# Two chained transformer blocks on one core: X and Y products in turns on four quarters of the array, and keys, norm scale and activations of the convolution kept in PSUM

## The chip, the core and the metric

The kernel runs on one core of a Trainium2 chip. The metric is the device time of one execution in microseconds. The kernel before has a median of 1738.71 us over 3 runs (1736.97 to 1738.91).

## What is computed

Two blocks run one after the other on 512 rows of 1024 features, all in fp32. The reference, cut down:

```python
def first_block(x, mem, ...):
    h, mem_h = rms_norm(x, norm_g), rms_norm(mem, mem_norm_g)
    c_glu, c_gate, d_q, d_k, d_v, d_gate, x_q, x_gate, merge = split(h @ w_in)
    y_conv = conformer_conv_branch(...)        # conv over 31 rows, layer_norm, silu(u) * silu(gate), @ w_proj
    y_diff = differential_attention_branch(...)
    y_mem = memory_cross_attention_branch(...) # rms_norm of q and k, softmax over 256 rows of mem, * silu(gate)
    g = sigmoid(merge)
    return x + (g[0] * y_conv + g[1] * y_diff + g[2] * y_mem) @ w_out

def second_block(x, c, ...):
    mod = silu(c) @ w_ada + b_ada              # six rows that scale and shift
    p = (x * (1 + sc1) + sh1) @ w_in
    mix = concatenate([gmlp_spatial_gating(p), rwkv7_time_mix(p)]) @ w_out
    x = layer_norm(ALPHA * x + gt1 * mix)
    ...                                        # FFN with silu gate, layer_norm

def _rwkv7_step(S, inp):                       # scanned over 512 rows, 8 heads of 64 x 64
    r, w, k, v, a, b = inp
    sa = einsum('bhij,bhj->bhi', S, a)
    S = S * w + sa[..., None] * b + v[..., None] * k
    return S, einsum('bhij,bhj->bhi', S, r)
```

## The kernel before

Each of the engines TensorE, VectorE, ACT and GpSimd has a program written out by hand, and semaphores hold them together. Matrices are multiplied in split form: every operand is kept as a high part and a rest, and `mm3` (L564 to L566) issues three products, hi by hi, lo by hi and hi by lo. Weights come in an order that `unit_plan` lists. One unit is 128 x 1024 of weights, which is 8 blocks of 3 products, 24 in all. It lands in one of four `raw` slots. ACT makes its high part (`weight_hi`, L599) as soon as the unit three places before it has been used. GpSimd makes its rest (`weight_lo`, L607) in the first part of the kernel, and VectorE in the later part. Units named `ada` are pieces of `w_ada`: VectorE multiplies them by the silu of c and sums them (L620), and TensorE takes no part.

The products go to eight PSUM banks, which are handed round by rings: a ring is a list of banks, and a tile that takes a bank waits until the earlier holder is released.

The first part, until the convolution's projection: the depthwise convolution runs on VectorE as 240 multiply-adds (L1993, `bank<-conv_in,columns,bank`). In between and behind it VectorE scales the keys of the memory (4 heads, each a pair of 256-column tiles in one bank, ring of banks 6 and 7) into scratch in SBUF, ACT copies their high part (L1500, `k_x_hi`), VectorE subtracts it (L1998, `k_x_lo`). The convolution is centred, squared and summed. Its norm scale r goes to a scratch tile by an exponential. For each of 8 tiles ACT then makes the silu in a scratch tile (ring of three places), VectorE multiplies by the gate, ACT copies the high part (L1444), VectorE subtracts (`branch_lo`, L1998) and scales the tile after next by r (`normed`, L1990, `conv_out<-conv_out,scratch`). Meanwhile TensorE works through four units of cross attention's head 0: query 0, query 1, gate 0, gate 1, in banks 2, 0, 1 and 2. The sum of the query's squares (`query_sum`, L957) stands in the middle of gate 0. Behind that come the units of the convolution's projection, from bank 0 on.

The RWKV part works in chunks of 64 rows. For each of four features f (a pair of heads) two triangular matrices V and Y are built up in six levels (L1233 and the lines behind it); `pe_squares` (L1190) issues 8 x 2 products of 64 x 64, one for each of 8 chunks m and two lane halves. Levels 1 to 4 have three such groups: V, then X = Y by V, then Y = V by Y. ACT copies X and Y to SBUF, VectorE masks V. Features 0 and 1 take turns, and then 2 and 3. [...]

Of the kernel before, what the change touches and what calls it, by code (L numbers as in the profile page):

```python
# [67 lines left out]
def unit_plan():  # L68
# [38 lines left out]
    for h in range(X_HEADS):  # L107
        for c in range(2):
            f(("xq", 2 * h + c), "w_in", W_IN_AT["xq"] + (2 * h + c) * P)
            if h:  # L110
                a()
        for c in range(2):
            f(("x_gate", 2 * h + c), "w_in", W_IN_AT["x_gate"] + (2 * h + c) * P)
            if h:
                a()
        if h == 0:
            for d in range(KT):
                f(("proj", 0, d), "w_conv_proj", d * P)
                a()
                if d % 2:  # L120
                    a()
    project(1, "w_x_proj")
    for h in range(HEADS):
        f(("dq", h), "w_in", W_IN_AT["dq"] + h * P)
        a()
        f(("dk", h), "w_in", W_IN_AT["dk"] + h * P)
        if h in DV_AT:
            t(("dv", DV_AT[h]), "w_in", W_IN_AT["dv"] + DV_AT[h] * 512)
        f(("d_gate", h), "w_in", W_IN_AT["d_gate"] + h * P)
    project(2, "w_diff_proj")  # L130
# [138 lines left out]
def build(nc, dram, out):  # L269
# [169 lines left out]
    silu_ring, norm_ring, norm_ring_q = place_ring((6, 7, 10)), place_ring((8, 9, 0, 1)), place_ring((8, 9))  # L439
# [423 lines left out]
    def pe_conv_mean(pe, n):  # L863
        bank = stats.take(pe, "mean", conv_centred, KT - 1) if n == 0 else stats["mean"]
# [79 lines left out]
    def pe_cross(pe):  # L944
# [18 lines left out]
        for h in range(X_HEADS):  # L963
# [6 lines left out]
            later = h > 0  # L970
            feature_unit(pe, ("xq", 2 * h), unit_bank(pe, ("xq", 2 * h)), h_T, mid=first_scores if later else None)
# [7 lines left out]
            feature_unit(pe, ("x_gate", 2 * h), unit_bank(pe, ("x_gate", 2 * h)), h_T, mid=query_sum)  # L979
            if later:  # L980
                pe_cross_value(pe, h - 1, 0)
            feature_unit(pe, ("x_gate", 2 * h + 1), unit_bank(pe, ("x_gate", 2 * h + 1)), h_T,
                         mid=second_value if later else None)
# [201 lines left out]
    def pe_squares(pe, bank, lhs, rhs, start=True):  # L1185

        for m in range(8):
            for part in range(2):
                lanes = cut(part, CHUNK)
                done = pe.matmul(bank[lanes, cut(m, CHUNK)], lhs(m, lanes), rhs(m, lanes), start=start,  # L1190
                                 stop=start or m == 7)
        return done

# [18 lines left out]
    def pe_chunks(pe, f):  # L1212
# [18 lines left out]
        for level in range(6):  # L1231
# [8 lines left out]
            pe_squares(pe, bank, masked(0, 0), table(X) if level else identity, start=False).then_inc(*pe_c.up(f, "V", level))  # L1240
# [6 lines left out]
            if level < 5:  # L1247
                bank = wide.take(pe, ("X", f, level), act_c, f, "X", level)
            else:
                bank = wide.take(pe, ("LkV", f), act_c, f, "LkV")  # L1250
                pe.wait_ge(*dve_c.at(f, "masked", 1, 1))
                pe.wait_ge(*act_f.at(f, "tok", 3))
                pe_squares(pe, bank, masked(1, 0), rows_of(V_tok)).then_inc(*pe_c.up(f, "LkV"))
            pe.wait_ge(*(act_c if level > 1 else dve_c).at(f, "Y", level - 1))
# [232 lines left out]
    def act_keys(act):  # L1487
# [85 lines left out]
    def act_cross(act):  # L1573
# [35 lines left out]
        for h in range(X_HEADS):  # L1609
# [7 lines left out]
            if later:  # L1617
# [3 lines left out]
                turns(h - 1, 1)  # L1621
            feed_hi(act)
# [6 lines left out]
            feed_hi(act)  # L1629
            gate(h, 0)  # L1630
# [444 lines left out]
    def dve_key_full(dve, h):  # L2075
        dve.wait_ge(*norm_r.at("xk", h))
        for c in (1, 0):
            fused(dve, norm_ring["xk", h, c][:, 0:M], key_bank(h, c), column("x_kn_g", c),
                  norm_ring["xk", h, 0][:, 0:M], ALU.mult, ALU.mult).then_inc(*taken["dve"].up("xk", 2 * h + c))

    def dve_key_lo(dve, h):
        for c in range(2):
            dve_rest(dve, k_x[1][:, 2 * h + c, :], norm_ring["xk", h, c][:, 0:M], k_x[0][:, 2 * h + c, :],
                     norm_hi.at("xk", h, c)).then_inc(*norm_lo.up("xk", h, c))

    def dve_keys(dve):
# [5 lines left out]
        def normed(n):  # L2092
            mult(dve, conv[:, n, :], conv[:, n, :], conv_r_ring[0]).then_inc(*conv_normed.up(n))

        def gated(n):
            dve.wait_ge(*conv_silu.at(n))
            mult(dve, silu_ring[n], silu_ring[n], conv_gates[:, n, :]).then_inc(*conv_gated.up(n))
            if n + 2 < KT:
                normed(n + 2)
            if n:  # L2100
                dve_branch_lo(dve, "conv", n - 1, silu_ring[n - 1])
# [670 lines left out]
```

## Time and profile before

| what | value |
|---|---|
| median of the runs | 1738.71 us |
| the profiled execution's own time | 1738.34 us |
| its span | 1736.6 us |
| TensorE busy | 1627.2 us (94%) |
| VectorE busy | 1003.6 us (58%) |
| ACT busy | 723.5 us (42%) |
| GpSimd busy | 192.7 us (11%) |
| granted TensorE clock, mean | 0.978 |

The span is what the profile covers, and the kernel's own time is 1.7 us more. TensorE's share is a mean over all stages: where it is busy, only shorter work helps, and where it is not, the releaser of its wait counts.

### The profile page before, as it was taken

To read this page: it belongs to the slowest core of one execution; us is meant where nothing else is said; L and a number is where in the kernel's file an instruction comes from. 1 tells how busy PE (TensorE), PEld (TensorE's weight loads), DVE (VectorE), ACT (ScalarE), POOL (GpSimd) and SP (SyncE) were. 2 spreads that over 40 slices of the span, in tenths; PEclk is the share of its full clock that TensorE was granted. 3 is DMA by queue.
4 is the path that set the end of the run, shared out by engine and by line. 5 is a ranking of instruction groups with operands and counts; after the bars stand their busy time and mean duration, and the time that the engine had idled before them with its cause. 6 is when DMAs were issued, how large, how long until landed. Compare 5 with 4: busy or idle time off the path is not lost. (4 is left out here: it accounts for less than half of the span.)

```text
span 1736.6 us, 24246 instructions
## 1 busy us (share of the span) xinstructions
PE 1627.2 (94%) x9944; PEld 1283.6 (74%) x9944; DVE 1003.6 (58%) x1644; ACT 723.5 (42%) x1145; POOL 192.7 (11%) x158
## 2 busy tenths in 40 slices
PE   6999989999999999899999899999888999999995
PEld 5777776788787766677788686788666887887883
DVE  5999976666655476566444647675437443332227
ACT  5543346344522476467522635553325222222111
POOL 2343335400010000000005000000000000000000
PEclk9999999999999999999999999999989999999998
DMA  5222323654465322221333232200012332222321
GB/s 199 97 85 74 97 85 121 199 178 145 137 181 154 98 79 72 79 91 61 122 97 117 86 103 73 73 4 4 3 37 75 107 118 88 91 92 85 97 73 48
DMA packets 45644, 166.07 MB, mean 96 GB/s; under 512 B 5264, under 2 KB 5392, under 8 KB 45536
## 3 DMA queue, kind: packets, MB, share of 16 engines
q1 hardware_dynamic: 42912, 155.95, 28.0%
q0 software_dynamic: 2624, 8.59, 1.6%
q8 instruction: 79, 1.29, 0.3%
q14 instruction: 29, 0.24, 0.0%
HBM read 162.42 MB, written 2.10 MB: 95 GB/s over the span
## 5 line engine op out<-in xcount | busy, mean ns | idle before, releaser
L607 DVE TENSOR_TENSOR weight_lo<-raw,weight_hi 128x1024 fp32r<-128x1024 f32 x184 | 225.6, 1226 | 487.7 <-ACT weight_hi L599 487.7
L564 PE MATMUL bank<-h_T_hi,weight_hi 128*128 128x512 f32 x1208 | 496.3, 411 | 5.5 <-DVE h_T_lo L1998 3.4
L599 ACT ACTIVATE weight_hi<-raw 128x1024 fp32r<-128x1024 f32 x241 | 254.5, 1056 | 569.9 <-PE bank L566 567.2
L565 PE MATMUL bank<-h_T_lo,weight_hi 128*128 128x512 f32 x1208 | 480.2, 397 | 0.0
L566 PE MATMUL bank<-h_T_hi,weight_lo 128*128 128x512 f32 x1208 | 479.9, 397 | 0.0
L564 PEld LDWEIGHTS bank<-h_T_hi,weight_hi 128*128 128x128 f32 x1208 | 229.0, 190 | 70.7 <-issue 11.6
L565 PEld LDWEIGHTS bank<-h_T_lo,weight_hi 128*128 128x128 f32 x1208 | 228.8, 189 | 55.6 <-issue 5.6
L566 PEld LDWEIGHTS bank<-h_T_hi,weight_lo 128*128 128x128 f32 x1208 | 228.6, 189 | 55.2
L1993 DVE SCALAR_TENSOR_TENSOR bank<-conv_in,columns,bank 128x512 f32<-128x512 f32 x240 | 181.4, 756 | 8.3
L607 POOL TENSOR_TENSOR weight_lo<-raw,weight_hi 128x1024 fp32r<-128x1024 f32 x57 | 141.3, 2485 | 205.5 <-ACT weight_hi L599 205.5
L566 PE MATMUL bank<-branch_hi,weight_lo 128*128 128x512 f32 x192 | 75.9, 396 | 0.0
L564 PE MATMUL bank<-branch_hi,weight_hi 128*128 128x512 f32 x192 | 75.9, 396 | 0.0
L565 PE MATMUL bank<-branch_lo,weight_hi 128*128 128x512 f32 x192 | 75.9, 396 | 0.0
L564 PE MATMUL bank<-weight_hi,hidden_hi 128*128 128x512 f32 x176 | 70.4, 400 | 3.4 <-DVE scratch L1990 2.4
L620 DVE SCALAR_TENSOR_TENSOR raw<-raw,silu_row 128x1024 f32<-128x1024 f32 x48 | 69.5, 1452 | 5.9 <-DMA raw<-in_weights 5.9
L565 PE MATMUL bank<-weight_lo,hidden_hi 128*128 128x512 f32 x176 | 70.2, 399 | 0.0
L566 PE MATMUL bank<-weight_hi,hidden_lo 128*128 128x512 f32 x176 | 70.1, 398 | 0.0
L564 PE MATMUL bank<-weight_hi,h_T_hi 128*128 128x512 f32 x160 | 63.4, 396 | 3.0 <-DVE scratch L1993 3.0
L566 PE MATMUL bank<-weight_hi,h_T_lo 128*128 128x512 f32 x160 | 63.2, 395 | 0.0
L565 PE MATMUL bank<-weight_lo,h_T_hi 128*128 128x512 f32 x160 | 63.2, 395 | 0.0
L575 ACT ACT_TABLE_LOAD x45 | 57.7, 1283 | 3.4 <-issue 2.6
L752 POOL DMA_DIRECT2D ln_rows<-in_ln_g x4 | 2.2, 546 | 410.4 <-DVE scratch L1990 329.6
(442 smaller groups left out, 2324.2 us busy)
## 6 DMA issues: line engine op xcount, KB each, us to landing
raw<-in_weights SPq DMA_DIRECT2D x289, 512.0 KB, 3.5
x_in<-in_x SPq DMA_DIRECT2D x4, 512.0 KB, 5.4
x_rows<-in_x POOLq DMA_DIRECT2D x4, 512.0 KB, 4.9
out<-x_rows SPq DMA_DIRECT2D x4, 512.0 KB, 2.6
mem_in<-in_mem POOLq DMA_DIRECT2D x2, 512.0 KB, 8.0
ln_rows<-in_ln_g POOLq DMA_DIRECT2D x4, 256.0 KB, 3.9
ln_rows<-in_ln_b POOLq DMA_DIRECT2D x4, 256.0 KB, 4.5
silu_row<-in_c POOLq DMA_DIRECT2D x1, 512.0 KB, 11.0
```

The costliest lines, as they stand in the source:

```text
L564: pe.matmul(o, lhs[0], rhs[0], start=start, stop=False)
L565: pe.matmul(o, lhs[0], rhs[1], start=False, stop=False)
L566: return pe.matmul(o, lhs[1], rhs[0], start=False, stop=stop)
L575: return act.activation(o, i, func, bias=bias, scale=scale)
L599: act.activation(parts[n % SPLIT][0][:, :], raw[u % RAW][:, :], ACT.Copy).then_inc(*weight_hi.up(u))
L607: engine.tensor_tensor(lo[:, :], raw[u % RAW][:, :], view(hi[:, :]), ALU.subtract).then_inc(*ready.up(u))
L620: dve.scalar_tensor_tensor(out=slot, in0=slot, scalar=1.0, in1=silu_row[:, :], op0=ALU.mult, op1=ALU.mult, accum_out=mod[:, v, k:k + 1]).t ...
L752: pool.dma_start(ln_rows[half][:, :], dram[f"{name}_g"][:, cut(half, 512)].broadcast_to([P, 512])).then_inc(*rows_loaded.up(name, half, 0))
L1993: return dve.scalar_tensor_tensor(out=o, in0=a, scalar=scalar, in1=b, op0=op0, op1=op1)
```

## The change

It has four parts.

1. In the plan, head 0's units come in the order gate 0, query 0, query 1, gate 1. Four `ada` pieces leave the projection and stand behind the gate of every second head in the differential stage.
2. PSUM. The keys' ring gets a third bank (6, 7, 1); the keys are normed in their bank, read there for high part and rest, and the bank is free once the rest is made. The convolution's norm scale is written to bank 3, which held the mean. The silu tiles are in banks 6 and 7. ACT waits for the last centred tile before it writes the scale, and for the keys' last rest before the first silu. The rest of tile n-1 now comes ahead of the scaling of tile n+2 on VectorE.
3. `query_sum` stands in the middle of gate 1, and ACT makes the silu of gate 0 ahead of the query's squares.
4. In the RWKV levels 1 to 4, X and Y products alternate (`pe_level`) on four quarters of 64 x 64: X of a chunk's half reads one row half and writes one column half of its bank, and Y writes the other column half of another bank. V and Y are kept in the other half of the partitions from level 2 on (`crossed`, `turned`).

```diff
@@ unit_plan
     for h in range(X_HEADS):
-        for c in range(2):
+        if h == 0:
+            for name, n in (("x_gate", 0), ("xq", 0), ("xq", 1), ("x_gate", 1)):
+                f((name, n), "w_in", W_IN_AT[name] + n * P)
+        for c in range(2) if h else ():
...
             for d in range(KT):
                 f(("proj", 0, d), "w_conv_proj", d * P)
                 a()
-                if d % 2:
-                    a()
...
         f(("d_gate", h), "w_in", W_IN_AT["d_gate"] + h * P)
+        if h % 2 == 0:
+            a()
@@ rings
-    mem_places, key_places, key_sums = bank_ring((6, 7)), bank_ring((6, 7)), bank_ring((2,))
-    value_places, square_places = bank_ring((0, 1, 5, 4)), bank_ring((4,))
-    conv_places = ring([bank[:, :] for bank in banks[4:6]])
+    mem_places, key_places, key_sums = bank_ring((6, 7)), bank_ring((6, 7, 1)), bank_ring((2,))
+    value_places, square_places = bank_ring((0, 5, 1, 4)), bank_ring((4,))
+    conv_places, silu_ring = ring([bank[:, :] for bank in banks[4:6]]), ring([bank[:, :] for bank in banks[6:8]])
...
-    silu_ring, norm_ring, norm_ring_q = place_ring((6, 7, 10)), place_ring((8, 9, 0, 1)), place_ring((8, 9))
+    norm_ring, norm_ring_q = place_ring((8, 9, 0, 1)), place_ring((8, 9))
@@ TensorE
-        key_places.take(pe, ("xk", h), taken["dve"], "xk", 2 * h)
+        key_places.take(pe, ("xk", h), norm_lo, "xk", h, 1)
...
+            if h == 0:
+                feature_unit(pe, ("x_gate", 0), unit_bank(pe, ("x_gate", 0)), h_T)
...
             feature_unit(pe, ("x_gate", 2 * h + 1), unit_bank(pe, ("x_gate", 2 * h + 1)), h_T,
-                         mid=second_value if later else None)
+                         mid=second_value if later else query_sum)
...
+    def pe_level(pe, banks, Y, V, table, crossed):
+        for m in range(8):
+            for part in range(2):
+                rows = cut(part ^ crossed, CHUNK)
+                x_done = pe_square(pe, banks[0], table(Y), table(V), m, rows, cut(part, CHUNK))
+                y_done = pe_square(pe, banks[1], table(V), table(Y), m, rows, cut(1 - part, CHUNK))
+        return x_done, y_done
...
-            if level < 5:
-                pe_squares(pe, bank, table(Y), table(V)).then_inc(*pe_c.up(f, "X", level))
-            bank = wide.take(pe, ("Y", f, level), act_c, f, "Y", level)
-            pe_squares(pe, bank, table(V), table(Y)).then_inc(*pe_c.up(f, "Y", level))
@@ ACT
-                act.activation(k_x[0][:, 2 * h + c, :], norm_ring["xk", h, c][:, 0:M], ACT.Copy).then_inc(
-                    *norm_hi.up("xk", h, c))
+                act.activation(k_x[0][:, 2 * h + c, :], key_bank(h, c), ACT.Copy).then_inc(*norm_hi.up("xk", h, c))
...
-        act_root(act, r, square_places["conv_sq"], r, 1.0 / D, EPS5, conv_r.up())
+        act.wait_ge(*conv_centred.at(KT - 1))
+        act_root(act, stats["mean"], square_places["conv_sq"], r, 1.0 / D, EPS5, conv_r.up())
         values(0)
+        act.wait_ge(*norm_lo.at("xk", X_HEADS - 1, 1))
...
+            if h == 0:
+                gate(h, 0)
+                feed_hi(act)
             feed_hi(act)
             squares(h)
@@ VectorE
-            fused(dve, norm_ring["xk", h, c][:, 0:M], key_bank(h, c), column("x_kn_g", c),
+            fused(dve, key_bank(h, c), key_bank(h, c), column("x_kn_g", c),
...
-            dve_rest(dve, k_x[1][:, 2 * h + c, :], norm_ring["xk", h, c][:, 0:M], k_x[0][:, 2 * h + c, :],
-                     norm_hi.at("xk", h, c)).then_inc(*norm_lo.up("xk", h, c))
+            dve_rest(dve, k_x[1][:, 2 * h + c, :], key_bank(h, c), k_x[0][:, 2 * h + c, :],
+                     norm_hi.at("xk", h, 1)).then_inc(*norm_lo.up("xk", h, c))
...
-            mult(dve, conv[:, n, :], conv[:, n, :], conv_r_ring[0]).then_inc(*conv_normed.up(n))
+            mult(dve, conv[:, n, :], conv[:, n, :], stats["mean"]).then_inc(*conv_normed.up(n))
```

Three places of the order. First TensorE at head 0's query sum. Before, it stands in the middle of the third unit, gate 0, in bank 1 (`h_T` are the rows, `weight2` the third pair of weight slots):

```order
L566 MATMUL bank1<-h_T_hi_79,weight2_lo_58 128x512
L957 MATMUL bank3<-scratch_more0_86,ones_all_68 128x512
L957 MATMUL bank3<-scratch_more1_87,ones_all_68 128x512
L564 MATMUL bank1<-h_T_hi_79,weight2_hi_57 128x512
L565 MATMUL bank1<-h_T_lo_80,weight2_hi_57 128x512
```

With the change the same two products stand in the fourth unit, gate 1, in bank 2:

```order
L567 MATMUL bank2<-h_T_hi_79,weight0_lo_54 128x512
L958 MATMUL bank3<-scratch_more0_86,ones_all_68 128x512
L958 MATMUL bank3<-scratch_more1_87,ones_all_68 128x512
L565 MATMUL bank2<-h_T_hi_79,weight0_hi_53 128x512
L566 MATMUL bank2<-h_T_lo_80,weight0_hi_53 128x512
```

The sum has moved by one unit of 24 products; 12 products and no more lie between it and the projection.

Second, ACT in the silu loop, the last tiles. Before, silu goes to scratch tiles 6, 7 and more2 in turn, and the high part is read from there:

```order
L575 ACTIVATE scratch6_65<-conv_out_81,columns_70 128x512
L1444 ACTIVATE branch_hi_83<-scratch_more2_88 128x512
L599 ACTIVATE weight1_hi_55<-raw1_50 128x1024
L575 ACTIVATE scratch7_66<-conv_out_81,columns_70 128x512
L1444 ACTIVATE branch_hi_83<-scratch6_65 128x512
L599 ACTIVATE weight2_hi_57<-raw2_51 128x1024
L575 ACTIVATE scratch_more2_88<-conv_out_81,columns_70 128x512
```

With the change the same instructions write and read banks 6 and 7:

```order
L576 ACTIVATE bank7<-conv_out_81,columns_70 128x512
L1465 ACTIVATE branch_hi_83<-bank6 128x512
L600 ACTIVATE weight1_hi_55<-raw1_50 128x1024
L576 ACTIVATE bank6<-conv_out_81,columns_70 128x512
L1465 ACTIVATE branch_hi_83<-bank7 128x512
L600 ACTIVATE weight2_hi_57<-raw2_51 128x1024
L576 ACTIVATE bank7<-conv_out_81,columns_70 128x512
```

The order stays; three places have become two.

Third, TensorE at level 1 of feature 0. Before, X's 16 products come first and Y's 16 behind them:

```order
L1225 MATMUL bank4<-AR_161,k_T_162 64x128
L1225 MATMUL bank5<-AR_161,k_T_162 64x128
L1190 MATMUL bank6<-V0_166,Y0_167 64x64 x16
L1190 MATMUL bank7<-Y0_167,V0_166 64x64 x16
L1225 MATMUL bank0<-AR_161,k_T_162 64x128
```

With the change they alternate, 32 rows of which the first five:

```order
L1241 MATMUL bank5<-AR_161,k_T_162 64x128
L1190 MATMUL bank6<-V0_166,Y0_167 64x64
L1190 MATMUL bank7<-Y0_167,V0_166 64x64
L1190 MATMUL bank6<-V0_166,Y0_167 64x64
L1190 MATMUL bank7<-Y0_167,V0_166 64x64
L1190 MATMUL bank6<-V0_166,Y0_167 64x64
```

The number of products is the same, and X's result is complete one product ahead of Y's, where it was 16 ahead.

## Rows read from the trace of the kernel before

**Rows 1.** The page, part 1: busy us, share of the span, instructions.

```profile
PE 1627.2 (94%) x9944; PEld 1283.6 (74%) x9944; DVE 1003.6 (58%) x1644; ACT 723.5 (42%) x1145; POOL 192.7 (11%) x158
```

**Rows 2.** TensorE's waits, whole kernel: us in total, times, longest.

```profile
PE bank L564 <- DVE scratch L1993: 8.5, 2, 5.5
...
PE bank L957 <- ACT scratch_more L1590: 4.4, 1, 4.4
```

**Rows 3.** Stretches on TensorE: its busy us, granted clock, DMA share, GB/s.

```profile
core 0: us, PE busy (x), PEclk, DMA share, GB/s
...
239.76:245.54 5.78, 0.28 (x4) 0.77 0.22 82
...
245.54:249.54 4.00, 4.00 (x18) 0.50 0.00 0
...
287.70:301.70 14.00, 14.00 (x60) 1.00 0.36 114
```

**Rows 4.** Timeline of VectorE and GpSimd at the keys; line L1993, all.

```profile
230.13 4.92 POOL L607 TENSOR_TENSOR weight_lo<-raw,weight_hi 128x1024 fp32r<-128x1024 f32 x2 [4.29 <-ACT weight_hi L599]
...
231.29 4.04 DVE L1998 TENSOR_TENSOR k_x_lo<-scratch_more,k_x_hi 128x256 fp32r<-128x256 f32 x2
...
245.96 0.76 DVE L1998 TENSOR_TENSOR k_x_lo<-scratch,k_x_hi 128x256 fp32r<-128x256 f32 x2 [0.48 <-ACT k_x_hi L1500]
...
L1993 DVE SCALAR_TENSOR_TENSOR bank<-conv_in,columns,bank x240: 744/756/759, 35.9 to 243.9; 128x512 f32<-128x512 f32 x120
```

**Rows 5.** Timeline of VectorE and GpSimd in the silu loop.

```profile
279.38 8.18 POOL L607 TENSOR_TENSOR weight_lo<-raw,weight_hi 128x1024 fp32r<-128x1024 f32 x3 [4.68 <-ACT weight_hi L599]
...
280.04 2.43 DVE L1990 TENSOR_TENSOR scratch<-scratch,conv_gates 128x512 f32<-128x512 f32 x1 [0.36 <-ACT scratch L575]
...
293.86 2.89 DVE L1990 TENSOR_TENSOR scratch<-scratch,conv_gates 128x512 f32<-128x512 f32 x1
...
301.49 0.68 DVE L1998 TENSOR_TENSOR branch_lo<-scratch,branch_hi 128x512 fp32r<-128x512 f32 x1
```

**Rows 6.** Timeline of ACT, VectorE and TensorE at the query's root.

```profile
310.36 0.69 ACT L575 ACTIVATE scratch_more<-bank,eps 128x512 f32<-128x512 f32 x1 [3.45 <-PE bank L957]
...
311.81 1.41 DVE L1993 SCALAR_TENSOR_TENSOR scratch_more<-bank,x_gain,scratch_more 128x512 f32<-128x512 f32 x2 [6.77 <-ACT scratch_more L575]
...
315.37 1.28 ACT L575 ACT_TABLE_LOAD   x1
...
318.97 0.40 PE L564 MATMUL bank<-branch_hi,weight_hi 128*128 128x512 f32 x1
```

**Rows 7.** Timeline of VectorE in the differential stage.

```profile
639.34 1.22 DVE L620 SCALAR_TENSOR_TENSOR raw<-raw,silu_row 128x1024 f32<-128x1024 f32 x1
...
656.00 1.23 DVE L607 TENSOR_TENSOR weight_lo<-raw,weight_hi 128x1024 fp32r<-128x1024 f32 x1 [2.12 <-ACT weight_hi L599]
```

**Rows 8.** Timeline of TensorE in the RWKV part.

```profile
1143.09 1.10 PE L1190 MATMUL bank<-V,Y 64*64 64x64 f32 x32
...
1144.02 1.10 PE L1190 MATMUL bank<-Y,V 64*64 64x64 f32 x32
...
1174.69 0.33 PE L1295 MATMUL bank<-tok0v,tok0k 64*64 64x64 f32 x8
...
1174.81 0.32 PE L1293 MATMUL bank<-AL,LM0a 64*64 64x64 f32 x8
```

**Rows 9.** Timeline of VectorE and ACT between the levels.

```profile
1140.82 0.17 DVE L2508 COPY small<-scratch 128x8 f32<-128x8 f32 x1
...
1145.95 0.63 ACT L575 ACTIVATE scratch<-scratch 128x512 f32<-128x512 f32 x1 [4.37 <-DVE scratch L2516]
...
1159.47 0.74 DVE L1993 SCALAR_TENSOR_TENSOR f_kk<-k_T,columns,scratch 128x512 f32<-128x512 f32 x1
...
1164.63 0.68 DVE L1990 TENSOR_TENSOR V<-bank,levels 128x512 f32<-128x512 f32 x1
...
1227.85 0.63 ACT L1956 ACTIVATE y_b<-k_T 128x512 fp32r<-128x512 f32 x1 [1.35 <-DVE k_T L1990]
```

More of the change, by code:

```diff
@@ L119, in unit_plan @@
                 a()
-                if d % 2:
-                    a()
     project(1, "w_x_proj")
@@ L129, in unit_plan @@
         f(("d_gate", h), "w_in", W_IN_AT["d_gate"] + h * P)
+        if h % 2 == 0:
+            a()
     project(2, "w_diff_proj")
@@ L863, in pe_conv_mean @@
     def pe_conv_mean(pe, n):
-        bank = stats.take(pe, "mean", conv_centred, KT - 1) if n == 0 else stats["mean"]
+        bank = stats.take(pe, "mean", conv_normed, KT - 1) if n == 0 else stats["mean"]
         pe.wait_ge(*conv_done.at(n))
@@ L1183, in pe_tokens, with pe_square, pe_squares @@
                 yield
-    def pe_squares(pe, bank, lhs, rhs, start=True):
+    def pe_square(pe, bank, lhs, rhs, m, rows, lanes, start=True):
+        return pe.matmul(bank[lanes, cut(m, CHUNK)], lhs(m, rows), rhs(m, rows), start=start, stop=start or m == 7)
+    def pe_squares(pe, bank, lhs, rhs, start=True, crossed=False, turned=False):
         for m in range(8):
             for part in range(2):
-                lanes = cut(part, CHUNK)
-                done = pe.matmul(bank[lanes, cut(m, CHUNK)], lhs(m, lanes), rhs(m, lanes), start=start,
-                                 stop=start or m == 7)
-        return done
+                done = pe_square(pe, bank, lhs, rhs, m, cut(part ^ crossed, CHUNK), cut(part ^ turned, CHUNK), start)
+        return done
+    def pe_level(pe, banks, Y, V, table, crossed):
[5 more added lines that the diff above has]
+        return x_done, y_done
     def chunk_parts(f):
@@ L1239, in pe_chunks @@
                 pe.wait_ge(*act_c.at(f, "X", level - 1))
-            pe_squares(pe, bank, masked(0, 0), table(X) if level else identity, start=False).then_inc(*pe_c.up(f, "V", level))
+            pe_squares(pe, bank, masked(0, 0), table(X) if level else identity, start=False, turned=level > 1).then_inc(
+                *pe_c.up(f, "V", level))
             yield
@@ L1247, in pe_chunks @@
             if level < 5:
[L1248 to L1254, printed above, removed]
+                pair = wide.take(pe, ("X", f, level), act_c, f, "X", level), wide.take(pe, ("Y", f, level), act_c, f, "Y", level)
+                pe.wait_ge(*(act_c if level > 1 else dve_c).at(f, "Y", level - 1))
+                pe.wait_ge(*dve_c.at(f, "V", level))
+                x_done, y_done = pe_level(pe, pair, Y, V, table, level > 1)
+                x_done.then_inc(*pe_c.up(f, "X", level))
+                y_done.then_inc(*pe_c.up(f, "Y", level))
+                yield
+                continue
+            bank = wide.take(pe, ("LkV", f), act_c, f, "LkV")
+            pe.wait_ge(*dve_c.at(f, "masked", 1, 1))
+            pe.wait_ge(*act_f.at(f, "tok", 3))
+            pe_squares(pe, bank, masked(1, 0), rows_of(V_tok)).then_inc(*pe_c.up(f, "LkV"))
+            bank = wide.take(pe, ("Y", f, level), act_c, f, "Y", level)
+            pe.wait_ge(*act_c.at(f, "Y", level - 1))
             pe.wait_ge(*dve_c.at(f, "V", level))
-            if level < 5:
-                pe_squares(pe, bank, table(Y), table(V)).then_inc(*pe_c.up(f, "X", level))
-            bank = wide.take(pe, ("Y", f, level), act_c, f, "Y", level)
-            pe_squares(pe, bank, table(V), table(Y)).then_inc(*pe_c.up(f, "Y", level))
+            pe_squares(pe, bank, table(V), table(Y), crossed=True).then_inc(*pe_c.up(f, "Y", level))
             yield
@@ L1628, in act_cross @@
             query_hi(h)
-            feed_hi(act)
-            gate(h, 0)
+            if later:
+                feed_hi(act)
+                gate(h, 0)
             if later:
```

12 lines of the change are left out of this document (5 added, 7 removed).

## The prediction, made before the changed kernel ran

> **What bounds the kernel now.** I read the page first: TensorE is busy for 1627.2 us, 94% of the span of 1736.6 [rows 1]. So only two things move the time: a TensorE wait that shrinks, or TensorE work that gets shorter. The list of TensorE's waits came next. The wait for a key tile is 5.5 us in one piece and the wait for the query squares 4.4 us [rows 2]; the largest in the RWKV part is shorter. The table of stretches then shows what such a wait costs behind it: after the 5.78 us without work, the next unit takes 4.00 us at a granted 0.50 [rows 3]. At the full clock 14.00 us hold 60 products, 0.233 us each, so a unit of 24 is 5.6 us [rows 3]. A key product has half the columns, 0.117 us, so its unit of 24 is 2.8 us, and the half clock cost 1.2.
>
> **The key stage.** Key tile pair 3 is written to the bank that pair 1 holds; with three banks it takes the bank that pair 0 left. That removes the 5.5 us wait itself, but TensorE then waits for the weight of the second unit. How early is that? VectorE's lo of pair 0 took 4.04 us for two instructions while GpSimd split weights from 230.13, and 0.76 for the same two at 245.96 [rows 4]. All 240 instructions of the convolution, whose inputs are one tensor in SBUF, one in PSUM and a column, stay within 744 to 759 ns though GpSimd splits weights beside them [rows 4]. So an instruction with two inputs in SBUF is held up by GpSimd and one with a PSUM input is not. The keys' lo now reads PSUM: 3.3 us less, and with it comes all that stands behind it on VectorE and then on the others: the convolution's last 12 instructions, pair 1's keys, ACT's copy of them, the split of the weight that ACT does next, GpSimd's lo of it. The second unit, which starts at 249.54 in the stretch table [rows 3], can start 3.1 us earlier, at 246.4 (I leave 0.2 for the reads of PSUM). TensorE ends the first, 239.9 + 2.8, at 242.7 and waits 3.7 us; now the second unit runs at the full clock from 249.54 on, but after a wait of 3.7 us some of it may run at half. A full unit of that costs 1.2; I take 0.7, as the wait is shorter. Gain at the end of the keys: 3.1 - 0.7 = **2.4 us** (bounds 1.9 and 3.1).
>
> **The convolution's activations.** From 280.04 to 296.7 five of VectorE's instructions with two SBUF inputs are lengthened, the first to 2.43 us and the others to 2.89 as the last, against 0.68, while GpSimd works 8.18 us on three weights and more behind them [rows 5]. Excess: 2.43 + 4 x 2.89 - 5 x 0.68 = 10.6 us. ACT's silu waits for the scratch place that these free. With activations, norm scale and lo in PSUM every such instruction has one SBUF input, so the 10.6 us go. The last gated product of the loop ends at 301.5; without the excess it is near 291, and I take the same with two places in place of three, since each is handed on as soon as its two readers are done. The extra waits (last centred tile ahead of the root; last key lo ahead of silu 0; mean bank) are all met before the query units run: nothing.
>
> **The query stage.** The sum waits 4.4 us for ACT's squares [rows 2], which stand behind the silu loop; they are then early, made right after query 1. The sum sits in the middle of the fourth unit in place of the third. Units start at 287.70 - 2.4 = 285.3 [rows 3]; the sum begins at 285.3 + 3.5 x 5.6 = 304.9, and with 1 us for its two products ends at 305.9, the fourth unit at 308.7. But silu of gate 0 is now ahead of the squares, so the root needs a table load, which waits for the sum: 1.28 us for the load, 1.45 for logarithm and exponential (310.36 to 311.81), 1.41 for VectorE's two instructions, and 0.3 at each of four hand-overs: 311.2 [rows 6]. The convolution's first projection unit now takes bank 0, which VectorE's second instruction frees; before it starts, at 318.97, they are long done [rows 6]. So TensorE waits 2.5 us, and starts at **311.2 in place of 318.97: 7.8 us** for the whole first part. Upper bound: without that wait and without half clock at the keys, 7.8 + 2.5 + 0.7 = 11. Lower: the wait of 2.5 us is followed by as much lost to half clock, 5.3.
>
> **The moved pieces of w_ada.** Four leave the projection, where TensorE waits for none of them, and go to four heads of the differential stage. Each is 1.22 us of VectorE there [rows 7]. VectorE sits 2.12 us idle before the lo that follows [rows 7], so I take nothing. Without that cover it is 4 x 1.22 = 4.9 us slower. Their DMAs move with them, the same number.
>
> **The products X and Y.** 16 levels issue 32 of them each. The trace shows 32 records in 0.93 us (1143.09 to 1144.02), two records a product: 16 products, 58 ns each. They use two of four quarters of the array. Where this kernel has all four quarters in turns, in the chunks' outputs, the next line's 8 records start 0.12 us after the 8 before: four products take that, 29 ns each [rows 8]. So X and Y together go from 1.87 to 0.93 us, 16 x 0.93 = **14.9 us** at most. What the rest gives back, by the order of the instructions: for features 0 and 1 VectorE is at other work until 1140.99, and the first mask would be wanted some 0.5 us before; ACT's X copy stands behind an exponential at 1145.95 that waits for VectorE (1.35 us); and VectorE runs 5.2 us of other work from 1159.47 before the mask of level 5 (V at 1164.63), 1.6 us late [rows 9]. 7.5 - 0.5 - 1.35 - 1.6 = 4.1. For features 2 and 3 ACT copies y_b ahead of X at 1227.85 [rows 9]: 7.5 - 0.7 = 6.8. Together **10.9 us** (bounds: 14.9, and 7 if each of the 8 pairs of levels gave another 0.5 back).
>
> The Trainium skill speaks against this term: "TensorEngine Tiling (Array Packing)", section "Restrictions and Gotchas", has it that different row tiles cannot access the same PSUM bank at once. X's two parts come from two row halves, and write one bank, before and after. Rows 8 already show 58 ns for two row halves that write one bank; no row shows four quarters on two banks in which each bank is written from both row halves. By the rule nothing of the 14.9 us would come, which is rival B.
>
> **Sum.** 7.8 + 10.9 + 0 = 18.7 us off the span of 1736.6: 1717.9. The profiled run's own time is 1738.34, so 1719.6, and the median of the runs is 0.4 above that run: **1720.0 us**. No change within 0.2% is 3.5 us.
>
> **Rivals.**
> A, the forecast: 0.62. Own range by the bounds: 1738.7 - 25.9 = 1713 to 1738.7 - 12.3 = 1726.
> B, quarters in turns bring nothing, as matmuls from different row halves to one bank take turns: 7.8 alone, 1730.9. For it: no row has the case. Against it: 58 ns for two row halves in one bank [rows 8]. 0.10.
> C, the products halve but VectorE's and ACT's copies set the pace. A level needs V product, mask, X/Y product, two copies (0.69 + 0.6 + 0.6 us and hand-overs) and the X copy used to run beside the Y product. Then most of the 10.9 is lost: 1727 to 1731. Against it: two features take turns, so that a level of the other stands between a product and its copy's reader. 0.12.
> D, the moved pieces sit on VectorE's path in the differential stage: +4.9, 1725. 0.06.
> E, the other side: the four quarters don't overlap at all where both row halves share a bank in turns, and each product takes 117 ns in place of 58, as much as two. 512 x 58 ns = +30 us, so 1738.7 - 7.8 + 30 = 1761, slower. It decides from 58 + 7.8/512 = 73 ns a product on. Against it: every product row of the stretch is 58 or 29 [rows 8]. 0.05.
> F, the first part gains nothing (ACT into PSUM slower, two places too few, the wait at the projection long enough for half clock): 1738.7 - 10.9 = 1728. 0.05.
>
> **Range.** 1713 to 1731 holds A, B, most of C, D and F and leaves out E. Faster by over 0.2%: all but E and mishaps of several at once, 0.91; same 0.03; slower 0.06.
>
> **What would show it.** Right: rows of L1190's successor with X and Y at 29 ns a product (32 records each inside 0.93 us); no VectorE instruction of 2.9 us between 270 and 300; waits of 5.5 and 4.4 gone, one of about 3.7 before the last key unit, one of 2 to 3 at the first product of the projection, which starts near 311; in RWKV new waits on ACT's X copy and on V, about 4 us in all. Wrong: those RWKV waits at 8 us or more (C), spacing of 58 (B) or 117 (E); a VectorE wait of over 1 us more at each even differential head (D).

## The result, and the profile after

The changed kernel takes 1720.65 us (median of 4 runs, 1720.13 to 1721.15), the kernel before 1737.84 in the same comparison (4 runs). The ratio is 0.9901, 95% interval 0.9884 to 0.9918. The forecast was 1720.0 us, faster, with a range of 1713 to 1731.

The page of the changed kernel, part 1:

```profile
span 1718.6 us, 24264 instructions
...
PE 1610.7 (94%) x9944; PEld 1269.0 (74%) x9944; DVE 983.8 (57%) x1644; ACT 723.9 (42%) x1147; POOL 190.2 (11%) x158
```

TensorE is busy 16.5 us less than in [rows 1], VectorE 19.8 us less, and the span is 18.0 us shorter. The list of TensorE's waits in the changed kernel (us in total, times, longest; all lines have moved, L564 is now L565, L1993 is L2019, and L607 is L608):

```profile
PE bank L565 <- POOL weight_lo L608: 4.9, 4, 2.5
...
PE bank L1190 <- DVE V L2016: 4.0, 2, 3.0
...
PE bank L1320 <- issue: 3.0, 2, 2.1
PE bank L1190 <- issue: 3.0, 3, 1.4
...
PE bank L1314 <- issue: 1.5, 1, 1.5
...
PE bank L565 <- DVE scratch_more L2019: 1.4, 1, 1.4
...
PE bank L1190 <- DVE LM0k L2016: 1.1, 1, 1.1
```

The 5.5 and the 4.4 us of [rows 2] are gone. A wait for GpSimd's weight of 2.5 us and one of 1.4 us at the projection are there; both were forecast, at 3.7 and 2.5 us. Three rows say "issue", in which TensorE waits for nothing that the profile shows. They sum to 7.5 us, and two of their three lines are in the chunks' last products, the third among the level products. Before there were 3.8 us of them in the chunks. The forecast had no such term.

The first part, on the timeline of TensorE, VectorE and ACT of the changed kernel (start us, us, engine, line, instruction, idle before):

```profile
231.16 0.75 DVE L2024 TENSOR_TENSOR k_x_lo<-bank,k_x_hi 128x256 fp32r<-128x256 f32 x2
...
234.86 0.39 PE L565 MATMUL bank<-mem_T_hi,weight_hi 128*128 128x256 f32 x1 [0.69 <-ACT y_T L576]
...
246.19 0.58 PE L565 MATMUL bank<-mem_T_hi,weight_hi 128*128 128x256 f32 x1 [2.55 <-POOL weight_lo L608]
...
279.35 0.70 DVE L2016 TENSOR_TENSOR bank<-bank,conv_gates 128x512 f32<-128x512 f32 x1 [0.26 <-ACT bank L576]
279.96 0.68 DVE L2024 TENSOR_TENSOR branch_lo<-bank,branch_hi 128x512 fp32r<-128x512 f32 x1
280.56 0.68 DVE L2016 TENSOR_TENSOR conv_out<-conv_out,bank 128x512 f32<-128x512 f32 x1
...
291.55 1.28 ACT L581 ACT_TABLE_LOAD   x1
...
306.25 1.28 ACT L571 ACT_TABLE_LOAD   x1 [2.41 <-PE bank L958]
...
310.46 0.50 PE L565 MATMUL bank<-branch_hi,weight_hi 128*128 128x512 f32 x1 [1.45 <-DVE scratch_more L2019]
```

The rests of key pair 0 take 0.75 us in place of 4.04 [rows 4]. No instruction of the silu loop is lengthened (compare [rows 5]), and the loop is over at 291.55, when ACT loads its next table. The last key unit starts at 246.19, forecast 246.4. The projection starts at 310.46, forecast 311.2, before 318.97 [rows 6]. From the sum at 304.34 on, the path is ACT's table load behind the sum, root, VectorE, projection.

The row at 234.86 is a wait that the kernel before doesn't have and the forecast left out: ACT still reads the third bank of the keys, bank 1, for `y_T`, and the last four key units start 0.69 us late. The traces of the ten kernels below that have the third bank all show it, and those of e1_levels and e8_double_before, which have two, don't. The first part, as measured below, starts behind this wait.

In the levels X and Y products alternate. One pair of groups, the first of feature 1, begins so; its 64 records start from 1130.79 to 1131.73:

```profile
1130.79 0.24 PE L1190 MATMUL bank<-V,Y 64*64 64x64 f32 x1 [1.09 <-DVE LM0k L2016]
1130.80 0.27 PE L1190 MATMUL bank<-Y,V 64*64 64x64 f32 x1
1130.81 0.27 PE L1190 MATMUL bank<-V,Y 64*64 64x64 f32 x1
1130.81 0.27 PE L1190 MATMUL bank<-Y,V 64*64 64x64 f32 x1
1130.87 0.22 PE L1190 MATMUL bank<-V,Y 64*64 64x64 f32 x1
1130.90 0.22 PE L1190 MATMUL bank<-Y,V 64*64 64x64 f32 x1
```

64 records are 32 products, two records each, in 0.94 us: 29 ns each, half of the 58 in [rows 8].

**Where the 18.0 us came from, by the starts of the same instructions in both traces.** The projection begins 8.5 us earlier. From there to the chunks 0.75 is lost. The chunks (first product of AL to the last) take 112.5 us in place of 119.8: 7.2. Behind them another 1.9 is gained, and 1.2 more later on. The table of stretches of the changed kernel (us, TensorE's busy us, granted clock, DMA share, GB/s) has two places where the clock does it:

```profile
712.00:722.00 10.00, 8.39 (x30) 0.83 0.16 54
```

```profile
1233.70:1267.00 33.30, 24.64 (x171) 15.10 (x161) 11.34 (x26) 7.48 (x15) 0.00 (x0) 0.85 0.00 1
```

The first of them has 1.00 in the kernel before, and the second 0.76, in 35.1 us. Such stretches come out differently in the kernels below, which don't touch them: the second takes 33.1 us in e1_levels and 35.3 in e4_sbuf. They are the chance of one execution: the changed kernel profiled a second time (e12_again) takes 1.9 us longer in the second stretch, 4.1 us longer from the projection to the end, and has a span of 1721.5 against 1718.6.

### The profile page after: what moved, and what is told of

Read it like the earlier page. It is cut to its first block and busy times, and to the rows that moved or that the text cites. A ratio compares the mean times of both kernels' runs of the same rounds, so it can differ in the third digit from the quotient of the medians.

```text
span 1718.6 us, 24264 instructions
## 1 busy us (share of the span) xinstructions
PE 1610.7 (94%) x9944; PEld 1269.0 (74%) x9944; DVE 983.8 (57%) x1644; ACT 723.9 (42%) x1147; POOL 190.2 (11%) x158
## 5 line engine op out<-in xcount | busy, mean ns | idle before, releaser
L608 DVE TENSOR_TENSOR weight_lo<-raw,weight_hi 128x1024 fp32r<-128x1024 f32 x184 | 225.5, 1225 | 485.0 <-ACT weight_hi L600 485.0
L565 PE MATMUL bank<-h_T_hi,weight_hi 128*128 128x512 f32 x1208 | 496.4, 411 | 4.5 <-DVE h_T_lo L2024 2.4
L565 PEld LDWEIGHTS bank<-h_T_hi,weight_hi 128*128 128x128 f32 x1208 | 229.7, 190 | 66.9 <-issue 10.3
L2019 DVE SCALAR_TENSOR_TENSOR bank<-conv_in,columns,bank 128x512 f32<-128x512 f32 x240 | 181.4, 756 | 8.3
L608 POOL TENSOR_TENSOR weight_lo<-raw,weight_hi 128x1024 fp32r<-128x1024 f32 x57 | 138.6, 2437 | 199.9 <-ACT weight_hi L600 199.8
L565 PE MATMUL bank<-branch_hi,weight_hi 128*128 128x512 f32 x192 | 76.0, 396 | 1.4 <-DVE scratch_more L2019 1.4
L565 PE MATMUL bank<-weight_hi,hidden_hi 128*128 128x512 f32 x176 | 69.7, 396 | 3.4 <-DVE scratch L2016 2.4
L565 PE MATMUL bank<-weight_hi,h_T_hi 128*128 128x512 f32 x160 | 64.1, 401 | 3.0 <-DVE scratch L2019 3.0
L621 DVE SCALAR_TENSOR_TENSOR raw<-raw,silu_row 128x1024 f32<-128x1024 f32 x48 | 64.3, 1341 | 1.7 <-DMA raw<-in_weights 1.7
```

The lines of the kernel that those rows point to most:

```text
L565: pe.matmul(o, lhs[0], rhs[0], start=start, stop=False)
L608: engine.tensor_tensor(lo[:, :], raw[u % RAW][:, :], view(hi[:, :]), ALU.subtract).then_inc(*ready.up(u))
L621: dve.scalar_tensor_tensor(out=slot, in0=slot, scalar=1.0, in1=silu_row[:, :], op0=ALU.mult, op1=ALU.mult, accum_out=mod[:, v, k:k + 1]).t ...
L2019: return dve.scalar_tensor_tensor(out=o, in0=a, scalar=scalar, in1=b, op0=op0, op1=op1)
```

## The experiments

Three numbers stand for each run. "First part" is from the start of the last four key units on TensorE to the first product of the projection, "chunks" is the stretch above; both are from its trace.

| run | median us | first part | chunks | issue waits in the chunks |
|---|---|---|---|---|
| before | 1737.84 | 84.8 | 119.8 | 3.8 |
| changed | 1720.65 | 75.6 | 112.5 | 7.5 |
| e1_levels | 1727.34 | 83.9 | 112.0 | 6.6 |
| e2_first | 1732.10 | 75.8 | 120.3 | 4.4 |
| e3_grouped | 1727.97 | 74.3 | 116.3 | 4.3 |
| e4_sbuf | 1729.46 | 81.6 | 112.8 | 6.3 |
| e5_order | 1717.03 | 73.1 | 111.7 | 6.5 |
| e6_ada | 1721.58 | 75.7 | 111.4 | 7.2 |
| e7_double | 1747.66 | 75.6 | 138.1 | 17.7 |
| e8_double_before | 1764.24 | 83.5 | 149.5 | 3.7 |
| e9_table | 1717.24 | 73.0 | 111.6 | 6.7 |
| e10_feed | 1713.94 | 70.3 | 112.1 | 7.0 |
| e11_keys | 1725.25 | 79.2 | 112.1 | 7.7 |
| e12_again | 1721.35 | 75.6 | 113.0 | 6.4 |

The kernel before had a median of 1737.92 us in the comparison with e1 to e4, 1738.87 with e5 to e8 and 1739.00 with e9 to e12. The chunks take 111.4 to 113.0 us in all the kernels with undoubled products in turns, so a difference below about 1.5 us there isn't to be read.

### The levels alone, and the rest alone

e1_levels is the kernel before with `pe_level`, `crossed` and `turned`; e2_first is the changed kernel without them.

> The kernel before with part 4 alone (X and Y in turns on four quarters). If the parts are independent, as the forecast has it, this gives what the changed kernel gains between the first level and the end of the chunks, 7 to 9 us: about 1729.5 us. Rival (code): the chunks' stretch shows waits of 1 to 2 us without a releaser, 7 us in all in place of 3.8, each a multiple of 256 TensorE instructions after the one before. Rival (levels need the earlier start of the first part): under 4 us gained, above 1734.

> The changed kernel with X and Y as before (part 4 taken back). Independent parts: the projection starts at about 310.5 as in the changed kernel, the levels are as before, time 1729.5 to 1730.5. Rival (the gain of the first part is given back at half clock later): 1733 or more.

e1: 1727.34 us, ratio 0.9950 (0.9932 to 0.9968). The chunks are 7.7 us shorter, the first part is as before. That is the forecast's separation, with the medians 2 us below the expectation: the profiled run again has some 2 us of clock behind the chunks. The issue waits are 6.6 us, as the rival about code has it. e2: 1732.10 us, ratio 0.9966 (0.9953 to 0.9979), first part 9.0 us shorter and chunks as before. Of these 9 us only about 6 are in the median: the projection begins 7.9 us earlier than before, and by the first product of the chunks 1.6 of that are lost again. That stretch takes 809.0 to 811.9 us over all fourteen traces, 0.6 more in e12_again than in the first profile of the same kernel. The two ratios together give 0.9916, against 0.9901 (0.9884 to 0.9918) for both: independent within the intervals. Rival B (no gain in the products) is out.

### What the turns do, and what the layout

e3_grouped keeps the other half of the partitions but issues all X products first:

```diff
     def pe_level(pe, banks, Y, V, table, crossed):
         for m in range(8):
             for part in range(2):
                 rows = cut(part ^ crossed, CHUNK)
                 x_done = pe_square(pe, banks[0], table(Y), table(V), m, rows, cut(part, CHUNK))
+        for m in range(8):
+            for part in range(2):
+                rows = cut(part ^ crossed, CHUNK)
                 y_done = pe_square(pe, banks[1], table(V), table(Y), m, rows, cut(1 - part, CHUNK))
```

> The changed kernel with V and Y in the other half of the partitions, but all 16 X products ahead of the 16 Y products. If the turns of the four quarters are what pays: 58 ns a product again and the time of the kernel without part 4, about 1729 to 1731. Rival (the layout itself, or X and Y overlap without turns): as the changed kernel, 1720 to 1722.

The expectation was wrong. The chunks take 116.3 us: 4.0 of the 7.8 us between e2 and the versions in turns are there without any turns. TensorE's timeline of this run, two features' levels one behind the other:

```profile
1142.99 0.97 PE L1190 MATMUL bank<-V,Y 64*64 64x64 f32 x26
1143.75 0.27 PE L1190 MATMUL bank<-Y,V 64*64 64x64 f32 x2
...
1143.92 0.80 PE L1190 MATMUL bank<-Y,V 64*64 64x64 f32 x21
1144.54 0.27 PE L1190 MATMUL bank<-V,Y 64*64 64x64 f32 x2
...
1144.71 0.80 PE L1190 MATMUL bank<-V,Y 64*64 64x64 f32 x21
1145.30 0.27 PE L1190 MATMUL bank<-Y,V 64*64 64x64 f32 x2
```

Where X's group ends, Y's products already start among X's last ones, since they use the other two quarters: a group takes 0.76 to 0.79 us in place of 0.93. Two groups are 1.55 us, against 1.87 before and 0.93 in turns. So 16 x 0.32 = 5.1 us is the layout's nominal part and 16 x 0.62 = 9.9 that of the turns; 4.0 and 3.8 arrive. Of what is missing from the turns, 3.2 us are issue waits (7.5 in the changed kernel, 4.3 here), to which the next experiment turns.

### Is it code that the short products wait for?

TensorE's "issue" waits have no releaser. I counted TensorE's instructions in the trace (weight loads, products, and the semaphore instructions between them) from one to the next:

```
changed:          1138.30 -> 1168.42: 1791   -> 1187.76: 1024   -> 1195.31: 512    -> 1229.10: 1793   -> 1233.27: 255
e12_again:        1137.9  -> 1169.2:  1791   -> 1195.9:  1536   -> 1229.3:  1793   -> 1233.2:  255
```

All are multiples of 256, give or take one. The DMA view shows code arriving in pieces of 16 KB; its row for one of the queues, for the whole of the changed kernel and then of e7_double (described below), is:

```profile
q8 instruction: 79, 1.29, 0.3%
```

```profile
q8 instruction: 87, 1.43, 0.3%
```

That queue is TensorE's: TensorE has 20355 instructions in the changed kernel, 79.5 times 256, and e7_double has 2048 more, 8 times 256.

e7_double and e8_double_before issue every X and Y product of levels 1 to 4 twice, into the same place:

```diff
 e7, pe_level
-            for part in range(2):
+            for part in (0, 1, 0, 1):
 e8, pe_chunks
+                pe_squares(pe, bank, table(Y), table(V))
                 pe_squares(pe, bank, table(Y), table(V)).then_inc(*pe_c.up(f, "X", level))
             bank = wide.take(pe, ("Y", f, level), act_c, f, "Y", level)
+            if level < 5:
+                pe_squares(pe, bank, table(V), table(Y))
```

> The changed kernel with every X and Y product of levels 1 to 4 issued twice into the same place (512 more products). If loading of code sets the pace where products are short, the waits without a releaser grow from 7.5 us to 15 or more, each a multiple of 256 instructions behind the last, and the chunks take over 18 us longer. If those waits are something else, the chunks take 12 to 15 us longer (512 x 29 ns = 14.9, less waits for data that it covers) and these waits stay near 7.

> The kernel before with every X and Y product of levels 1 to 4 issued twice. Products take 58 ns there, so 256 instructions, 64 products, take 3.7 us. Both theories: 27 to 31 us more. Code loading: waits without a releaser stay under 6 us, as a block of instructions lasts about as long as it takes to come. If the products are cheaper than 58 ns when they follow each other at once: under 25.

Waits of e7_double on TensorE around the chunks, and the code in its DMA view of the same 142 us:

```profile
PE bank L1190 <- issue: 13.7, 12, 1.8
...
PE bank L1320 <- issue: 2.5, 2, 1.5
PE bank L1314 <- issue: 1.5, 1, 1.5
```

```profile
q8 instruction: 32, 0.52, 1.6%
```

The chunks take 25.6 us more than in the changed kernel, where the products alone are 14.9. Issue waits are 17.7 us in 15 pieces, and the counts between them are 512, 256, 512, 767, 1024, 1025, 255, 512, 256, 768, 512, 512, 513 and 255. Where two follow at once (1140.8 and 1144.7, 1200.8 and 1204.6, 1212.3 and 1216.3, 1256.3 and 1259.9) the 256 instructions take 3.6 to 4.0 us, wait included, though 64 products of 29 ns are 1.9 us. In e8_double_before 64 products of 58 ns are 3.7 us, the chunks take 29.7 us more (512 x 58 ns = 29.7), and the issue waits stay at 3.7. (Its median is only 25.4 us above the kernel before, under the 27 expected: some 4 us came off in the first part and behind the chunks, which the edit doesn't touch.)

So a block of 256 TensorE instructions takes about 3.8 us to come, and products of 29 ns use it up in half the time. That the block is fetched code follows from counts, rate and the size of the pieces, and from when the pieces start. In all fourteen traces every issue wait in the chunks, over 80 together, ends 2.2 to 2.9 us after the latest piece has started, and in e7_double, between waits that follow at once, a piece starts every 3.6 to 4.0 us. The issue wait of 5.2 us that every trace has behind the chunks is no such wait: it ends 14 to 16 us after a piece, and 338 instructions behind the wait before it in the changed kernel. Still, no run changed the fetching itself.

The Trainium skill, "Runtime: NRT & Kernel Launch", section "Instruction fetch mechanics", has the block (16 KiB, 256 instructions), and this trace agrees. It also says that the fetch is hidden, because instructions are issued more slowly than they arrive. This case's trace doesn't agree: TensorE waits 7.5 us of the chunks, and 17.7 with the products doubled.

### Is it GpSimd, and PSUM?

e4_sbuf puts the silu tiles back into SBUF, three places; the norm scale stays in PSUM. e11_keys puts the scaled keys back; banks and releases stay as changed.

```diff
 e4
-    conv_places, silu_ring = ring([bank[:, :] for bank in banks[4:6]]), ring([bank[:, :] for bank in banks[6:8]])
+    conv_places = ring([bank[:, :] for bank in banks[4:6]])
+    silu_ring = place_ring((6, 7, 10))
 e11
-            fused(dve, key_bank(h, c), key_bank(h, c), column("x_kn_g", c),
+            fused(dve, norm_ring["xk", h, c][:, 0:M], key_bank(h, c), column("x_kn_g", c),
 (key_hi and dve_key_lo read norm_ring["xk", h, c] in place of key_bank(h, c))
```

> The changed kernel with the silu tiles back in SBUF, three places; the norm scale stays in PSUM. If GpSimd holds up VectorE instructions with two SBUF inputs, several of the gated products and rests between 275 and 300 take 2.4 to 2.9 us again, the silu loop ends 4 to 8 us later and the projection starts 3 to 6 us later: 1723 to 1727. Rival (it is the order and the squares' early place, not PSUM, that bought the time): within 1 us of the changed kernel.

> The changed kernel with the scaled keys in SBUF again (banks and releases stay). If GpSimd holds up an instruction with two SBUF inputs: the two rests of pair 0 take 4 us in place of 0.75, the last key unit waits 5 to 6 us in place of 2.55, and 2 to 3.5 us are lost, 1723 to 1724. Rival (only the third bank mattered): within 1 us of the changed kernel.

VectorE's timeline of e4_sbuf:

```profile
276.76 2.29 DVE L2016 TENSOR_TENSOR scratch<-scratch,conv_gates 128x512 f32<-128x512 f32 x1 [0.36 <-ACT scratch L576]
278.97 2.89 DVE L2024 TENSOR_TENSOR branch_lo<-scratch,branch_hi 128x512 fp32r<-128x512 f32 x1
281.79 0.67 DVE L2016 TENSOR_TENSOR conv_out<-conv_out,bank 128x512 f32<-128x512 f32 x1
282.38 2.29 DVE L2016 TENSOR_TENSOR scratch_more<-scratch_more,conv_gates 128x512 f32<-128x512 f32 x1
```

and TensorE's waits of the same run between 236 and 330 us:

```profile
PE bank L565 <- DVE v_x_lo L2024: 3.5, 1, 3.5
PE bank L565 <- DVE scratch_more L2019: 1.4, 1, 1.4
```

Five instructions take 2.3 to 2.9 us, and all five have two inputs in SBUF. The scaling by the norm scale, one input of which is now in PSUM, takes 0.67 to 0.68 each time, between them and in the same kernel. The loop ends some 5 us later, VectorE's rest of the values with it, and the third unit waits 3.5 us for the bank that it frees, at a place that I hadn't thought of, and runs at a granted clock of 0.52 for 3.3 us behind it. The first part is 6.0 us longer and the projection 4.8 us later, inside the expectation. The median, 1729.46 us, is 8 to 9 more than the changed kernel and 2 above the expectation; those further 2 to 3 us lie behind the projection, where the trace takes as long (1412.5 us) as that of e12_again (1412.3). e11_keys, VectorE and TensorE's waits between 236 and 330 us:

```profile
231.47 4.02 DVE L2024 TENSOR_TENSOR k_x_lo<-scratch_more,k_x_hi 128x256 fp32r<-128x256 f32 x2
```

```profile
PE bank L565 <- POOL weight_lo L608: 7.4, 3, 5.8
```

The two rests take 4.02 us again, and the last key unit waits 5.8 us in place of 2.55, 3.3 more, which is 4.02 less 0.75. The first part is 3.6 us longer, 1725.25 us against 1721.35 on the same chip. By the times alone the two aren't apart (1722.36 to 1727.03, and 1716.13 to 1725.10); the trace is what shows the cause. It also shows what the third bank does without PSUM keys: the last key unit starts at 249.83, where before it started at 249.54 [rows 3]. The bank alone buys nothing there; it is the shorter rests that bring the weight sooner. The keys in PSUM on two banks weren't tried.

So both PSUM edits pay through the same thing: a VectorE instruction with two inputs in SBUF stands while GpSimd splits a weight (2.4 us each in e11_keys) and one with an input in PSUM doesn't. The Trainium skill, "SBUF — State Buffer", section "SBUF: two separate sides", has this as an exclusive lock of the port that both share. By that rule, the trace agrees: each of e4_sbuf's five instructions ends 0.55 us after one of GpSimd's splits ends, about what such an instruction takes alone (0.68).

### The new order of head 0, and its table load

e5_order takes back the order of the units, the place of the sum and that of ACT's first gate. e9_table keeps the new order, with one line:

```diff
             squares(h)
+            if h == 0:
+                exp_table(act)
```

> The changed kernel with head 0's units, the query sum and the silu of gate 0 in the order of before (queries, then gates, sum in the third unit). The forecast held the new order to cost a wait at the projection (2.5 us) and to win nothing that the shorter silu loop had not won: then the sum finds its squares done, the wait of 1.4 us at the projection and its table load are gone, and the projection starts 1.5 to 2 us earlier than at 310.46: about 1719. Rival (the new order is needed, ACT comes to the squares too late for a sum in the third unit): a wait of 2 us or more at the sum, and half clock behind it, 1722 or more.

> The changed kernel with one edit: ACT loads the table for the query's root right behind the squares, while TensorE still computes, in place of behind the sum. If the wait at the projection is the chain behind the sum, it falls from 1.45 us by the 1.28 of the load to 0.1 or 0.2, the projection starts 1.2 to 1.3 us earlier: about 1719.4. Rival (the wait is for bank 0 or the weight): unchanged.

TensorE's waits between 236 and 330 us (e9_table):

```profile
PE bank L565 <- POOL weight_lo L608: 4.2, 3, 2.6
PE bank L565 <- DVE scratch_more L2021: 0.2, 1, 0.2
```

e5: 1717.03 us, ratio 0.9881 (0.9864 to 0.9897). The sum finds its squares: TensorE waits neither there nor at the projection, and only 0.17 us at the start of the fourth unit, whose bank VectorE frees. e9: the wait at the projection is 0.16 in place of 1.45, the same 1.3 us, 1717.24 us, ratio 0.9881 (0.9855 to 0.9907). In both traces the first part is 2.5 us shorter, of which 1.3 is this wait and 1.3 the last key unit, which neither edit touches. Behind the same wait of 2.55 us that unit runs at full clock in e5_order and at half in the changed kernel, as the table of stretches shows, first of e5_order and then of the changed kernel:

```profile
245.01:248.80 3.79, 3.79 (x26) 1.00 0.56 156
```

```profile
246.19:249.00 2.81, 2.81 (x13) 0.50 0.56 178
```

That half is chance: behind this wait the unit ran at half clock in six of the nine traces that have it, e12_again among them, and at full clock in e3, e5 and e9. So the new order of head 0 costs the changed kernel 1.3 us and gives nothing: in e5_order ACT has finished the squares at 295.8, and TensorE comes to the sum at 296.3. The difference of the medians, 3.6 to 4.1 us, is more than the trace explains, and the intervals overlap.

### The moved pieces of w_ada

> The changed kernel with the four pieces of w_ada back in the projection. Forecast: their place is worth nothing either way, the time within 1.5 us of the changed kernel. Rival (D, they sit on VectorE's path in the differential stage): 4 to 5 us faster than the changed kernel, 1716. Rival (they delayed the projection's weights): slower by over 2 us.

1721.58 us, ratio 0.9899 (0.9885 to 0.9914) against 0.9901 and 0.9896: nothing, as forecast. TensorE's waits in the differential stage are the same in both, row by row, the largest 5.4 us in 4 pieces. Rival D is out.

### A better version, and the repeat

e10_feed is e5_order with two lines of ACT exchanged, so that the weight split doesn't stand behind the copies of key pair 1, which wait for VectorE's convolution:

```diff
         root(1)
-        key_hi(1)
         feed_hi(act)
+        key_hi(1)
```

> The old order of head 0 (as in the fifth run) and on ACT the weight split ahead of the copies of key pair 1. If the wait of 2.55 us before the last key unit is that weight, split behind copies that wait for VectorE, the wait goes (at most 0.5 us left, at the sum of the convolution's last tile) and the keys end 2 to 3.5 us earlier, half clock included: 1714 to 1715.5. Rival (the centring waits for the convolution's last tile anyway): the wait moves to the sums behind it, less than 1 us gained, 1717.

> The changed kernel once more, on the same chip as the three others: 1720 to 1721.5, and waits in the chunks at the same multiples of 256 instructions apart.

ACT's timeline of e10_feed, and TensorE's waits between 236 and 330 us:

```profile
237.84 1.06 ACT L599 ACTIVATE weight_hi<-raw 128x1024 fp32r<-128x1024 f32 x1
241.88 0.66 ACT L1518 ACTIVATE k_x_hi<-bank 128x256 fp32r<-128x256 f32 x2 [2.98 <-DVE bank L2012]
```

```profile
PE bank L564 <- POOL weight_lo L607: 1.6, 2, 1.0
PE bank L564 <- DVE scratch_more L2012: 0.2, 1, 0.2
```

1713.94 us, ratio 0.9854 (0.9833 to 0.9875), the fastest of all. The 2.55 us wait is gone, and so is the chance of half clock behind it; the first part is 70.3 us. The repeat e12_again gives 1721.35 (0.9896, 0.9866 to 0.9926) and shows how far one execution wanders: its four runs reach from 1716.13 to 1725.10, and its span is 2.9 us above the first profile's, with the same first part.

## Why the prediction was right

**Mechanism of the first part: right, and nearly the size.** Forecast 7.8 us, measured 8.5 at the projection (9.2 over the first part alone). Keys: the last unit at 246.19 against 246.4; the wait before it 2.55 and not 3.7, since I had the unit ahead of it end at 242.7, and it ended at 243.6; 0.7 of that is the wait for bank 1, which the forecast left out. The half clock behind the wait cost 1.3 us, and I had 0.7. The rests' 3.3 us are e11's 3.3. Silu loop: end near 291 forecast, 291.55 measured; two places were enough. Query: 2.5 us of wait forecast at the projection, 1.45 measured. From the start of the sum to the projection the forecast had 6.3 us (304.9 to 311.2), and it took 6.1 (304.3 to 310.5); the wait is shorter because the sum holds TensorE for 1.3 us and not 1.0, and the unit ended at 309.0.

**The 10.9 us of the levels: right in kind, too large by 3.7.** The products halved to 29 ns as taken from [rows 8]: 14.9. The waits for data came to 3.1 us (1.0 V, 1.1 the mask of LM0, 0.4 Y, 0.6 AL), forecast 4.15: the exponential behind VectorE, for which I had 1.35, did not show, and the first mask cost 1.1 and not 0.5. What failed is the step "what the rest gives back, by the order of the instructions": it priced waits for data alone. Another 3.6 us (7.45 less 3.84) are the blocks of 256 instructions, for which the forecast had no term. A measured 7.2 is at the edge of the bounds that I gave, 7 and 14.9. Another microsecond is spread over gaps too short to list.

**The sum was better than its terms.** 8.5 + 7.2 = 15.7 us is what the two parts give; 2.3 more came from the granted clock in stretches that the change doesn't touch, and the forecast had 18.7. Part of the closeness of 1720.0 to 1720.65 is therefore chance: in the second profile of the same kernel such stretches made 4.1 us of difference behind the projection.

**w_ada: 0** forecast and measured. **The order of head 0**: I priced it inside the first part, where it is a loss of 1.3 us; e9 shows the upper bound of the forecast, which has neither that wait nor half clock at the keys: 11 us forecast, and its first part is 11.8 us shorter than before.

**Rivals.** B (no product gain) is out by e1; the rule on row tiles and one bank cost nothing here: with four quarters in turns each bank is written from both row halves, each half to its own partitions, and a product takes 29 ns. "TensorEngine Tiling (Array Packing)" of the Trainium skill, section "Restrictions and Gotchas", names it as a restriction; the measurement decides. C (ACT and VectorE set the pace) holds for 3.1 us of 14.9. D is out by e6, E by the spacing of 29 ns, F by the first part of e2, 9.0 us shorter.

## What to carry to other kernels

Products of different quarters overlap even without being issued in turns, where one group follows another in the free quarters, and turns then give the rest; but as products get short, count instructions: TensorE here took some 3.8 us per 256 of them, and a group that runs faster than that only moves its time to an unnamed wait. When VectorE and GpSimd both work in SBUF, put one of VectorE's two inputs into PSUM, if a bank is free, and look at who read that bank last: here the third bank brought a new wait of 0.7 us. And after a stall is removed, look again at reorderings made for its sake: here the reordered units cost 1.3 us, and one exchanged pair of ACT lines was worth more than them.

## What the runs showed of the hardware that I had not expected

- TensorE stops without a releaser, at multiples of 256 of its instructions, where they are used up faster than about 3.8 us per block, each time until 2.2 to 2.9 us after a piece of 16 KB of its code has started to arrive: 7.5 us in the changed kernel, 17.7 with doubled products, 3.7 where products take 58 ns.
- Two groups of 16 products of 64 x 64 on complementary quarters, one behind the other, take 1.55 us in place of 1.87.
- Two rests with both inputs in SBUF take 4.02 us beside GpSimd and 0.75 with one input in PSUM.
- The same wait of 2.55 us was followed by products at a granted clock of 0.50 in six traces (one every 213 ns) and of 1.00 in three (118 ns), which is 1.3 us of the time.
